# Output projections of a gated recurrence, taken by pairs of heads and half a weight slot a step

## The reference, cut to what matters

```python
q, k, g, v, z = hgrn_project(h, w_in, lb)             # five streams for each of 16 heads
o = chunk_scan(q, k[0], v, g[0], s_f) + flip(chunk_scan(flip(q), flip(k[1]), flip(v), flip(g[1]), s_b))
y = rms_norm_2(o, norm_g).astype(z.dtype) * silu(z)   # for each head
out = transpose(y).reshape(B, N, H * d) @ w_out       # (512 x 2048) @ (2048 x 1024)
```

## Time and profile before

| | us |
| --- | --- |
| median of 3 runs | 2565.55 (2564.66 to 2566.69) |
| the profiled execution | 2565.31 |
| its span | 2563.6 |
| around the span | 1.7 |
| TensorE busy, share of the span | 2414.8, 94% |
| mean granted TensorE clock | 0.98 of full |
| step 0 of the recurrence, first products of f0 to the end | 50.0 |
| steps 1 to 14, each | 58.7 |
| step 15 | 47.0 |

### The profile page before, as it was taken

One profiled execution on the slowest core, in us unless ns is written; L12 is line 12 of the kernel. 1 busy time (PEld: TensorE's weight loads), 2 busy tenths in 40 slices (PEclk: granted clock), 3 DMA queues, 4 the chain that ended last, 5 costly groups with the idle time before them and its releaser, 6 DMA issues.

```text
span 2563.6 us, 34914 instructions
## 1 busy us (share of the span) xinstructions
PE 2414.8 (94%) x12140; PEld 1994.4 (78%) x12140; DVE 1513.5 (59%) x2014; ACT 987.2 (39%) x1537; POOL 369.3 (14%) x499
## 2 busy tenths in 40 slices
PE   5999999789999999999999999999999997899997
PEld 4888887556787788888888888888888886688886
DVE  6666535465334666634666666666666665655545
ACT  3333323464332433333444434444444443432323
POOL 0111000000000111000133222333333332000000
PEclk8999999899999999999999999999999998899999
DMA  6666532111222566533211111111111110221221
GB/s 260 228 227 221 180 123 70 49 42 44 88 90 91 200 211 214 194 115 100 74 58 58 52 54 49 51 55 49 57 49 57 57 57 17 70 83 67 80 74 41
DMA packets 69512, 253.65 MB, mean 99 GB/s; under 512 B 7632, under 2 KB 7760, under 8 KB 69456
## 3 DMA queue, kind: packets, MB, share of 16 engines
q1 hardware_dynamic: 51312, 186.82, 21.8%
q0 software_dynamic: 18144, 66.07, 7.7%
HBM read 250.76 MB, written 2.10 MB: 99 GB/s over the span
## 4 chain that ended last, share of the span: by engine, by line
PE 82%; DVE 10%; ACT 3%; issue 3%; DMA 1%; DVEq 0%; ACTq 0%; POOL 0%; SPq 0%; POOLq 0%
PE ps L196 23%; PE ps L198 23%; PE ps L197 23%; PE ps L1157 4%; DVE xT L1495 3%; PE ps L1260 1%; PE ps L1248 1%; PE ps L312 1%; DVE nt L272 1%; PE ps L1246 1%; ACT wh L187 1%; DVE XL L1453 1%; PE ps L1256 1%; DVE wl L192 1%; PE ps L650 1%
## 5 line engine op out<-in xcount | busy, mean ns | idle before, releaser
L196 PE MATMUL ps<-hH,wh 128*128 128x512 f32 x1776 | 707.6, 398 | 19.1 <-DVE wl L192 9.8
L198 PE MATMUL ps<-hH,wl 128*128 128x512 f32 x1776 | 694.3, 391 | 0.0
L197 PE MATMUL ps<-hL,wh 128*128 128x512 f32 x1776 | 693.9, 391 | 0.0
L192 DVE TENSOR_TENSOR wl<-raw,wh 128x1024 fp32r<-128x1024 f32 x331 | 407.4, 1231 | 437.2 <-ACT wh L187 433.6
L187 ACT ACTIVATE wh<-raw 128x1024 fp32r<-128x1024 f32 x331 | 347.9, 1052 | 222.3 <-PE ps L198 147.2
L196 PEld LDWEIGHTS ps<-hH,wh 128*128 128x128 f32 x1776 | 335.1, 189 | 91.0 <-issue 15.7
L198 PEld LDWEIGHTS ps<-hH,wl 128*128 128x128 f32 x1776 | 334.5, 188 | 71.4
L197 PEld LDWEIGHTS ps<-hL,wh 128*128 128x128 f32 x1776 | 335.2, 189 | 65.7 <-issue 0.2
L1609 POOL TENSOR_TENSOR XR<-XR,fp 128x512 f32<-128x512 f32 x112 | 141.3, 1261 | 636.7 <-ACT KQ L1332 636.7
L521 POOL DMA_DIRECT2D araw<-in_ada x120 | 63.6, 530 | 922.2 <-ACT rs L252 415.6
L1330 ACT ACTIVATE KQ<-XL 128x512 f32<-128x512 f32 x112 | 72.2, 645 | 194.0 <-PE ps L1157 64.9
(11 more groups left out here) (298 smaller groups left out, 3832.8 us busy)
## 6 DMA issues: line engine op xcount, KB each, us to landing
raw<-in_ws SPq DMA_DIRECT2D x331, 512.0 KB, 3.2
araw<-in_ada POOLq DMA_DIRECT2D x120, 512.0 KB, 4.9
praw<-in_ada SPq DMA_DIRECT2D x16, 512.0 KB, 10.3
xin<-in_x SPq DMA_DIRECT2D x1, 2048.0 KB, 8.8
out_x<-xout SPq DMA_DIRECT2D x1, 2048.0 KB, 6.4
cin<-in_ctx POOLq DMA_DIRECT2D x1, 1024.0 KB, 5.1
traw<-in_dfts POOLq DMA_DIRECT2D x2, 512.0 KB, 4.1
cst<-in_const SPq DMA_DIRECT2D x1, 512.0 KB, 3.5
```

The costliest lines, as they stand in the source:

```text
L192: dve.tensor_tensor(wl[:, j, :], raw[:, j, :], wh[:, j, :].bitcast(F32), ALU.subtract).then_inc(lo_ready, 1)
L196: pe.matmul(o, a_hi, b_hi, start=start, stop=False, **kw)
L197: pe.matmul(o, a_hi, b_lo, start=False, stop=False, **kw)
L198: return pe.matmul(o, a_lo, b_hi, start=False, stop=stop, **kw)
```

## The change

The projection is taken by pairs of heads. A slot now holds half of the output tiles (four) of both heads of a pair. A step from 5 to 14 does one such slot: four tiles of two heads, 24 products, each tile summed in PSUM over the pair, so that x gets 4 additions a step instead of 8. Step 5 works on heads 0 and 1, so y is kept for six heads (`y0H`, `y4H`, `y5H` and their low halves; two of these lie in space that the context's halves and the mask leave free). Steps 1 to 4 have no projection. Step 14 has no z; the z stream of head 15 is computed in step 15, into bank 5. Step 15 has four half slots for pairs 5 and 6 (w0, w1, w2, w3: 96 products), with banks 0, 1, 2, 4. The end has two half slots, for heads 14 and 15; the products of head 14 go ahead, six of eight tiles before y of head 15 is there. The steps' hardware loop is written out on TensorE, ScalarE and VectorE (GpSimd keeps its loop). The number of slots is the same (96 for the recurrence), and so is that of projection products (384). The additions (L1495) are 56 instead of 128.

```diff
+        HG_PLAN, _s = [], S_HG + 5
+        for _i in range(HG):
+            _n = ("f0", "f1") + (("w",) if _i >= OUT_FROM else ()) + (("q", "z", "v") if _i < HG - 2 else ("q", "v"))
+            if _i == HG - 1:
+                _n = ("w0", "w1", "z", "w2", "w3")
...
-        OUT_BANKS = (0, 3, 5)
-        def out_pe(pe, s, r, n):
-            slot_ready(pe, s, r, 6)
-            pe.wait_ge(h_yl, n + 1)
+        OUT_BANKS = (0, 3, 5, 0)
+        END_BANKS = (0, 1, 2, 4)
+        def out_tile(pe, s, u, n, bank, start, stop):
             j = s % RING
-            for o in range(KD):
-                if o >= 3:
-                    pe.wait_ge(resid, at(HG_R + o - 2, n, 8))
-                w, b = slice(o * P, (o + 1) * P), OUT_BANKS[o % 3]
-                products(pe, ps[:, b, :], wh[:, j, w], wl[:, j, w], yH[:, :], yL[:, :], True, True).then_inc(h_w, 1)
-            pe.drain().then_inc(slot_done, 1)
+            w = slice((4 * (n % 2) + u) * P, (4 * (n % 2) + u + 1) * P)
+            return products(pe, ps[:, bank, :], wh[:, j, w], wl[:, j, w], Y_HI[n % 6], Y_LO[n % 6], start, stop)
...
+            else:
+                pe.wait_ge(h_kc, 3 * i)
+                pe.wait_ge(h_z, i)
+                slot_ready(pe, a["w0"])
+                pe.wait_ge(h_yl, 12)
+                for u in range(4):
+                    for n in (10, 11):
+                        out_tile(pe, a["w0"], u, n, END_BANKS[u], n == 10, False)
+                pe.drain().then_inc(slot_done, 1)
+            if i:
                 ms_pe(pe, i - 1)
...
+            else:
+                slot_ready(pe, a["w1"])
+                pe.wait_ge(h_yl, 14)
...
             scores_hg(pe, i, 0)
             value_pe(pe, i)
             scores_hg(pe, i, 1)
...
+            else:
+                pe.wait_ge(h_vc, 2 + 2 * i)
+                lat_pe(pe, a["z"], 5).then_inc(slot_done, 1)
             scores_hg(pe, i, 2)
-            if prev:
-                out_pe(pe, s + a["w"], r, i - 1)
+            if OUT_FROM <= i and more:
+                p = (i - OUT_FROM) // 2
...
+                pe.wait_ge(h_yl, 2 * p + 2)
+                for u in range(4):
+                    if u == 3:
+                        pe.wait_ge(resid, out_count(i) + 1)
+                    for n in (2 * p, 2 * p + 1):
+                        last = out_tile(pe, a["w"], u, n, OUT_BANKS[u], n == 2 * p, n == 2 * p + 1)
+                    last.then_inc(h_w, 1)
+                pe.drain().then_inc(slot_done, 1)
+            if not more:
+                slot_ready(pe, a["w2"])
+                for u in range(4):
+                    pe.wait_ge(resid, out_count(i) + u + 1)
...
+                if not more:
+                    for n in (12, 13):
+                        last = out_tile(pe, a["w3"], part, n, END_BANKS[part], False, n == 13)
+                    last.then_inc(h_w, 1)
...
                 if part < 3:
                     scores_hg(pe, i, 5 + part)
-            pe.wait_ge(resid, at(HG_R, i, 8))
+            pe.wait_ge(resid, out_count(i + 1) if more else HG_R + HG_OUT + 7)
```

At the end on TensorE, and on VectorE in a step and at the end:

```diff
-            ms_pe(pe, HG - 1)
-            out_pe(pe, S_HG + 6 * HG - 1, 0, HG - 1)
+            out_tile(pe, e, 0, last - 1, 0, True, False)
+            ms_pe(pe, last)
+            for o in range(1, 6):
+                out_tile(pe, e + o // 4, o % 4, last - 1, o, True, False)
+            pe.wait_ge(h_yl, HG)
+            for o in range(KD):
...
+                if o >= 6:
+                    out_tile(pe, e + 1, o % 4, last - 1, o, True, False)
+                out_tile(pe, e + o // 4, o % 4, last, o, False, True).then_inc(h_w, 1)
...
             place(dve, i, 2)
-            if prev:
-                for o in range(5):
-                    out_dve(dve, i - 1, o)
+            outs(0, 2)
             level_dve(dve, i, 3)
-            if prev:
-                for o in range(5, KD):
-                    out_dve(dve, i - 1, o)
-            split("w")
+            outs(2, 4)
...
             level_dve(dve, i, 6)
+            if not more:
+                for u in range(2):
+                    out_dve(dve, HG_OUT + 4 + u, 4 + u, END_BANKS[u])
             place(dve, i, 6)
+            if not more:
+                out_dve(dve, HG_OUT + 6, 6, END_BANKS[2])
             place(dve, i, 7)
...
             y_dve(dve, last)
-            split_lo(dve, S_HG + 6 * HG - 1 + LEAD)
             yl_dve(dve, last)
+            split_lo(dve, S_LAST + LEAD)
             for o in range(KD):
-                out_dve(dve, last, o)
+                if o == 5:
+                    split_lo(dve, S_LAST + 1 + LEAD)
+                out_dve(dve, HG_OUT + 8 + o, o, o)
```

More of the change, by code:

```diff
@@ L1089, in build @@
         HG_R = 24 + 2
+        OUT_FROM = 5
+        HG_OUT = 4 * (HG - 1 - OUT_FROM)
         def hcol(t, i, dr, h):
@@ L1215, in step_pe @@
                         w = slice(k * P, (k + 1) * P)
-                        last = products(pe, ps[:, 4, :], wh[:, z_j, w], wl[:, z_j, w], hH[:, k, :], hL[:, k, :], k == 0, k == KD - 1)
+                        last = products(pe, ps[:, 4, :], wh[:, j, w], wl[:, j, w], hH[:, k, :], hL[:, k, :], k == 0, k == KD - 1)
                     if part == 3:
                         last.then_inc(slot_done, 1)
+                if not more:
+                    for n in (12, 13):
+                        last = out_tile(pe, a["w3"], part, n, END_BANKS[part], False, n == 13)
+                    last.then_inc(h_w, 1)
+                    if part == 3:
+                        pe.drain().then_inc(slot_done, 1)
@@ L1366, in step_act @@
                 y_act(act, i - 1)
-            z_act(act, i)
+            if more:
+                z_act(act, i)
             value_copy_act(act, i)
+            if not more:
+                split("z")
             merge_act(act, i, 2)
             if more:
-                gates_act(act, s + a["f1"], r, i + 1, 1)
+                gates_act(act, a["f1"], i + 1, 1)
             merge_act(act, i, 3)
-            split("w")
+            if not more:
+                z_act(act, i)
+            split("w" if more else "w2")
             merge_act(act, i, 4)
@@ L1376, in step_act @@
                 split("q")
-                query_act(act, s + a["q"], r, i + 1)
+                query_act(act, a["q"], i + 1)
             merge_act(act, i, 5)
-            split("z")
+            if more:
+                split("z")
             merge_act(act, i, 6)
@@ L1387, in step_act @@
                 act.activation(dst, src, ACT.Copy).then_inc(h_kc, 1)
-            split("v")
+            split("v" if more else "w3")
             if more:
-                value_act(act, s + a["v"], r, i + 1)
+                value_act(act, a["v"], i + 1)
         def hg_act(act):
@@ L1510, in step_dve @@
             place(dve, i, 0)
-            split("f1")
+            split("f1" if more else "w1")
             level_dve(dve, i, 1)
@@ L1515, in step_dve @@
                 yl_dve(dve, i - 1)
-            z_dve(dve, i)
+            if more:
+                z_dve(dve, i)
+            else:
+                for u in range(4):
+                    out_dve(dve, HG_OUT + u, u, END_BANKS[u])
+                split("z")
             level_dve(dve, i, 2)
             place(dve, i, 2)
-            if prev:
-                for o in range(5):
-                    out_dve(dve, i - 1, o)
+            outs(0, 2)
             level_dve(dve, i, 3)
-            if prev:
-                for o in range(5, KD):
-                    out_dve(dve, i - 1, o)
-            split("w")
+            outs(2, 4)
+            if not more:
+                z_dve(dve, i)
+            split("w" if more else "w2")
             place(dve, i, 3)
             level_dve(dve, i, 4)
-            split("q")
+            if more:
+                split("q")
             place(dve, i, 4)
@@ L1534, in step_dve @@
             place(dve, i, 5)
-            split("z")
+            if more:
+                split("z")
             level_dve(dve, i, 6)
+            if not more:
+                for u in range(2):
+                    out_dve(dve, HG_OUT + 4 + u, 4 + u, END_BANKS[u])
             place(dve, i, 6)
+            if not more:
+                out_dve(dve, HG_OUT + 6, 6, END_BANKS[2])
             place(dve, i, 7)
-            split("v")
+            if not more:
+                out_dve(dve, HG_OUT + 7, 7, END_BANKS[3])
+            split("v" if more else "w3")
             states_dve(dve, i)
```

219 lines of the change are left out of this document (124 added, 95 removed).

## The result

The kernel after takes 2520.8 us at the median (2516.6 to 2522.2, 4 runs) against 2565.9 (2564.7 to 2566.7, 4 runs): ratio 0.982, interval 0.981 to 0.984, faster by 45 us. The profiled execution took 2522.2 with a span of 2520.5, so the two profiles differ by 43.1 us of span. It is the slowest of the four executions; the fastest took 5.6 us less.

A forecast was written before the change was run, and what follows sets the result against it. TensorE was taken to bound steps 0 to 14 and the chain of levels step 15. The terms 31.2 + 11.7 + 2.1 - 1.9 - 0.6 = 42.5 off 2565.3 gave 2522.8, stated as 2523 us; range 2511 to 2537.

The forecast's parts named there:

- Steps 1 to 4: Steps without a projection take step 0's form: 7.8 us gained each, 31.2 in all, bounds 6.8 and 8.08 a step.
- Steps 5 to 13: Half slots remove the 1.19 us wait ahead of the fourth tile: 1.3 a step, 11.7 in all, bounds 0 and 1.7.
- The 0.23 ahead of q may stay: In steps 5 to 13, q's 0.23 us wait may remain, since the fourth addition comes just as scores 3 end.
- Step 14: 1.3 us gained from the half slot plus 0.8 from leaving out z (bounds 0 and 5.57): 2.1.
- Step 15: 120 products for 24, placed by hand among the levels: step ends at 48.9, 1.9 us lost; bounds 5 gained, 8 lost.
- States and outputs at the full clock: Assumption for the end of step 15, by which the step ends at 48.9 us.
- The rule of the clock: TensorE's clock halves after idleness: 2523 if w0 to w3 keep it at work, up to 28 us more, 2551, if not.
- The end: Behind step 15, the second split stands among the additions, where VectorE bounds: 0.6 us lost, bounds 2 either way.
- The loop written out: Every step loads its code, some 65 instruction packets in all, fetched ahead: costed at nothing.
- the first (more comes back): Rival, chance 0.17: full 8.08 in steps 1 to 4, 1.7 in 5 to 13, step 15 no longer: about 52, 2513.
- The second (the last step's projections on the path): Rival, chance 0.17: projections lie on step 15's path or run at the low clock, losing 10 to 23 us; 2535.
- The third: Rival, chance 0.04: fetching the written-out code stalls TensorE, 125 us of stalls, slower than before at 2648.

The follow-up runs named there:

- e1: The kernel before with only its middle steps' loop written out on TensorE, ScalarE and VectorE: 2564.9 us, ratio 0.9992.
- e2: The kernel after with pairs only two or three steps behind, one half slot in step 15 and z kept in step 14: 2531.6 us, ratio 0.986.
- e7: The kernel after with z of head 15 back in step 14, its sigmoid on ScalarE ahead of the value copies: 2515.1 us, one run.
- e10: The kernel after, drain kept, with q in steps 5 to 14 waiting only for the second addition: 2517.1 us, one run.
- e5: The kernel after with eighteen idle products of 512 columns added on TensorE in step 15: 2518.3 us, one run.
- e8: The kernel after with z back in step 14 (sooner sigmoid), w3's additions earlier, no drain in steps 5 to 14, two w1 tiles behind scores 1: 2511.7 us.
- e9: e8 with q also waiting for the second addition only: 2506.5 us, ratio 0.976 against the kernel before.
- e4: The kernel after with VectorE's additions for w3 in step 15 each one link earlier: 2514.2 us, one run.

## Why the prediction was right, step by step

The forecast of 2523 stands 2 us above the median. Its sum is 42.5 and the profiles differ by 43.1, but two terms were mis-sized, one each way (6.7 more in steps 5 to 13, 4.0 less in step 15), and hid each other together with 3.8 us of scatter in untouched code. That the sum meets the measurement to 1 us is luck.

- **Steps 1 to 4 (31.2 forecast, 32.3 measured).** The step without a projection is step 0's form: 8.07 of the 8.08 came back, 0.15 of it by the loop (e1). The deduction of 0.3 a step for y of the head before was not needed: VectorE is busy for 32.80 of 50.70 us, and TensorE waits for nothing. e2 shows the same 50.66 for its step 1.
- **Steps 5 to 13 (11.7, 18.4).** The mechanism was right, the size wrong. The step that failed is "The 0.23 ahead of q may stay", with a restart counted once at most: the term was 1.3, its upper bound 1.7, and the measured value 2.05. Both waits went, and each took more than its length with it. Against e1, which has no loop, they gave 1.40 for 1.09 and 0.42 for 0.30, together 1.82 of the 1.90 between e1's step (58.58) and this one (56.68); the loop gave the other 0.15.
- **Step 14 (2.1, 2.1).** The sum is right and neither of its terms is, which is luck. The half slot gave 2.05 here as in the steps before, where the term was 1.3. Leaving out z gave nothing (56.68, as in steps 5 to 13), where the term was 0.8. That z gives little there, between 0 and 5.57, was the boldest choice, and it held; e7 shows it from the other side, with z put back at no cost. The reason held in half. The step's TensorE after:

```profile
2060.22 1.16 PE L1170 MATMUL ps<-KQ 128*128 128x128 f32 x8 [1.80 <-ACT KQ L1404]
2061.99 0.52 PE L1278 MATMUL ps<-cst,XL 128*128 128x128 f32 x3 [0.61 <-DVE XL L1532]
...
2063.34 0.69 PE L1287 MATMUL ps<-cst,XL 128*128 128x128 f32 x2 [0.27 <-POOL XR L1694]
...
2064.11 0.78 PE L198 MATMUL ps<-hH,wh 128*128 128x512 f32 x1
```

  What z leaves free becomes waits, but for the merges (1.80) and the last level (0.61) more than for GpSimd (0.27), for which the forecast had it wait. From scores 4 to the third transposes it is 8.54 us for 9.72 before (2054.80 to 2063.34; 1752.68 to 1762.40), so 1.2 came back. But the gaps had let the clock fall (0.97 in the step's window), and all of it went again: 0.4 in the transposes, and 0.8 in v, whose first products start 0.4 to 0.6 apart and only later 0.23, so that it takes 6.36 where such a slot takes 5.57. In e10 the clock held in this step (1.00), and there step 14 takes 55.49, 1.1 less than its steps 5 to 13. The forecast's 0.8 was sound for the levels; the clock was not in it.
- **Step 15 (1.9 lost, 5.9 lost).** The schedule by hand held up to the transposes: w0 to w2 and z in their places, w2 to 28.05 (forecast 27.3), scores 4 to 29.8 (29.0), the transposes at 40.8 (39.9), 1.71 late for the additions that the forecast had named as what bounds there. What failed is "States and outputs at the full clock": that makes 3.1 us (12.45 for the 9.35 of e5), which with the 0.9 up to the transposes is the 4.0 missing. The rule of the clock was weighed, and by it up to 28 us stood against the change; but I asked only whether w0 to w3 keep TensorE at work, and not what the clock does behind them, where TensorE waits 1.71, 0.69 and 1.93. The step's mean of 0.94 is above the 0.9 that I had set as the sign of a good outcome, and still cost 3 us.
- **The end (0.6 lost, 0).** As good as nothing either way: 26.54 for 26.53.
- **The loop written out (0, 2 gained).** e1: 0.15 a step, within the noise of the whole. In the table this is part of the steps' gains.

Of the rivals, the first (more comes back) was right in steps 1 to 13, which gave 50.7 where it had 47.6, and wrong in step 15, which did not keep its length. The second (the last step's projections on the path) is true in part: 8.2 of 22.3 us lie on it, but the step lost 5.9, below the 10 at which that rival began. The third is ruled out.

The trade between the two ends was therefore this. Taking 72 products out of steps 2 to 4 gave 18.0, since TensorE bounds there. Putting them, and z, into step 15 cost 8.2 (e2 against the kernel after): 9.4 up to the transposes, less 1.2 behind them. In e8, with the additions moved and with z in the gaps of step 14 as well, step 15 is shorter (43.50) than before the change (46.99), though it holds 96 products instead of 24.

**What stays open.** The clock in the last two steps differs between kernels that have the same code there: step 15 takes 43.50 in e8 and 45.09 in e9, 52.92 after and 51.42 in e10. Step 14 takes 56.68 after and 55.49 in e10, where only q's wait differs, which was worth at most 0.1 in the steps before. Each was profiled once, so I can't say whether this belongs to the kernel or to the execution. For the same reason what e4, e5 and e7 gained in step 15 (4.6, 3.0, 4.5) is known to some 1.6 us only.

## What to carry to other kernels

Work that is moved from a bound stage into an idle one should be costed link by link of the idle stage's chain: here 14 of 22 us hid, and of the rest 1.5 were the place of three small operations on another engine and 2.8 a stream (z) that would have been free in the step before. Cost the clock too, behind the last of the moved work: there it took up to 3.1 of 12.45 us. Where two waits stand one behind the other, as a drain and a bank's release do here, taking away either shows nothing, and both have to go in one kernel before either is called free. Filler that looks removable (z in step 14) may stand in another chain's gap: ask where it stands before you pay to put it elsewhere.

## What the runs showed of the hardware

A wait costs more than the idle time that the profile prints. In the middle steps of e1 a wait of 1.09 us was worth 1.40. The idle time is counted from the end of a record of 0.40, while in an unbroken row the next product starts 0.23 behind the start of the last; and the first product behind the wait holds TensorE for 0.33 instead of 0.23 (1744.05 to 1744.38), as it does behind scores. Together that is 1.36 of the 1.40.

In the chain-bound tail of step 15 the granted clock fell from 2.4 to 1.2 GHz though TensorE never waited for more than 1.93 us at a time (the waits were 1.71, 0.69 and 1.93): eight outputs took 1.91 for 1.06, and the tail 10.8 to 12.5 us in six kernels for 9.4 in three.

Work that computes nothing can pay: eighteen idle products shortened step 15 from 52.92 to 49.93, on one profile each. The Trainium skill (TensorE: Matmul & The Clock Gate, What's actually happening) calls the low clock the default that activity releases; e5 agrees, with a step mean of 1.00 for 0.94.

Stretches with the same code ahead of and behind the recurrence differed by up to 3.6 us between kernels (1220.2 to 1223.8 for the first product of the prologue), while the steps without gaps agreed to 0.1 us in 57.
